# Residual sums of seven of the eight pairs move from VectorE to GpSimd in two RMS-norm transitions of a two-block fp32 kernel

## What is computed

```python
m = jnp.concatenate([a, p], axis=-1) @ w_o[l]
x = x + rms_norm(m, post_mix_g[l])          # transition 1
h = rms_norm(x, pre_ffn_g[l])
up = causal_dwconv(h @ w_up[l], conv_w[l], conv_b[l])
y = (jax.nn.gelu(up[..., :D_FF], approximate=True) * up[..., D_FF:]) @ w_down[l]
x = x + rms_norm(y, post_ffn_g[l])          # transition 2
# second block:
xx = jnp.pad(x, ((0, 0), (1, 0), (0, 0)))[:, :-1] - x
xs = x[None] + xx[None] * mu_proj[:, None, None, :]
proj = jnp.einsum('sbtd,sde->sbte', xs, w_in)
```

## Time and profile before

| what | value |
|---|---|
| median of the runs (2199.85 to 2202.3) | 2200.96 us |
| the profiled execution's own time | 2203.91 us |
| its span, first to last instruction | 2202.1 us |
| TensorE busy | 2155.0 us (98%) |
| VectorE busy | 1486.4 us (67%) |
| ScalarE busy | 1080.2 us (49%) |
| GpSimd busy | 89.5 us (4%) |
| mean granted TensorE clock | 0.992 |

### The profile page before, as it was taken

The page is one execution under the profiler, slowest core; times in us unless marked ns, Lnnn a source line. Parts: engine busy times, 40 slices in busy tenths (PEclk is TensorE's granted clock), DMA queues, the critical chain, the costliest instruction groups (busy, mean ns, idle before and its releaser), DMA issues.

```text
span 2202.1 us, 38428 instructions
## 1 busy us (share of the span) xinstructions
PE 2155.0 (98%) x14720; PEld 1844.7 (84%) x14720; DVE 1486.4 (67%) x2059; ACT 1080.2 (49%) x1521; POOL 89.5 (4%) x78
## 2 busy tenths in 40 slices
PE   9999999999999999999899999999899999999997
PEld 7888888888888888888788888887788888888886
DVE  6556558886488866786786389884676544566655
ACT  5444555444444443444644666544434544556533
POOL 0700000000000000000000000001210000000000
PEclk9999999999999999999999999999999999999998
DMA  8655545665666656655455566653454655654552
GB/s 287 205 168 156 165 148 176 189 190 184 189 190 189 187 187 190 186 175 171 150 175 184 173 180 177 208 167 83 131 172 138 192 189 192 183 153 148 168 183 85
DMA packets 399585, 383.35 MB, mean 174 GB/s; under 512 B 43497, under 2 KB 397345, under 8 KB 398625
## 3 DMA queue, kind: packets, MB, share of 16 engines
q1 hardware_dynamic: 399458, 381.58, 56.1%
HBM read 374.65 MB, written 6.87 MB: 173 GB/s over the span
## 4 chain that ended last, share of the span: by engine, by line
PE 87%; DVE 8%; issue 2%; ACT 2%; DMA 1%; POOL 0%; DVEq 0%; SPq 0%; ACTq 0%; POOLq 0%
PE acc L800 46%; PE acc L803 23%; PE acc L831 3%; PE acc L886 2%; PE acc L887 2%; PE acc L888 2%; PE aux L1155 2%; DVE w_lo L2093 2%; PE acc L834 1%; PE aux L1081 1%; PE aux L903 1%; PE aux L1101 1%; ACT w_hi L1464 0%; DVE inverse L2529 0%; PE aux L1388 0%
## 5 line engine op out<-in xcount | busy, mean ns | idle before, releaser
L2093 DVE TENSOR_TENSOR w_lo<-raw_w,w_hi 128x1024 fp32r<-128x1024 f32 (+1 forms) x592 | 713.1, 1224 | 456.5 <-ACT w_hi L1464 454.8
L1464 ACT ACTIVATE w_hi<-raw_w 128x1024 fp32r<-128x1024 f32 (+1 forms) x592 | 613.5, 1046 | 673.2 <-PE acc L803 574.6
L800 PE MATMUL acc<-h,w_hi 128*128 128x512 f32 x1664 | 525.8, 397 | 1.2 <-DVE w_lo L2093 1.2
L803 PEld LDWEIGHTS acc<-h,w_lo 128*128 128x128 f32 x1664 | 312.6, 188 | 73.8
L803 PE MATMUL acc<-h,w_lo 128*128 128x256 f32 x1664 | 327.0, 278 | 0.0
L800 PEld LDWEIGHTS acc<-h,w_hi 128*128 128x128 f32 x1664 | 254.5, 189 | 2.2 <-issue 1.4
L800 PE MATMUL acc<-ff,w_hi 128*128 128x512 f32 x704 | 222.8, 398 | 2.4 <-DVE ff L2350 2.4
L800 PE MATMUL acc<-x_split,w_hi 128*128 128x512 f32 x704 | 225.1, 401 | 0.0
L800 PE MATMUL acc<-xs_b,w_hi 128*128 128x512 f32 x512 | 162.3, 398 | 1.7 <-DVE w_lo L2538 0.9
L803 PEld LDWEIGHTS acc<-ff,w_lo 128*128 128x128 f32 x704 | 133.0, 189 | 31.5
L803 PEld LDWEIGHTS acc<-x_split,w_lo 128*128 128x128 f32 x704 | 132.2, 188 | 31.2
(11 more groups left out here) (384 smaller groups left out, 3068.2 us busy)
## 6 DMA issues: line engine op xcount, KB each, us to landing
raw_w<-in_w_up SPq DMA_DIRECT2D x176, 512.0 KB, 3.5
raw_w<-in_a_w_in SPq DMA_DIRECT2D x128, 512.0 KB, 4.1
raw_w<-in_w_in SPq DMA_DIRECT2D x64, 512.0 KB, 4.1
raw_w<-in_w_down SPq DMA_DIRECT2D x64, 512.0 KB, 3.6
raw_w<-in_b_w_qg SPq DMA_DIRECT2D x64, 512.0 KB, 3.8
raw_w<-in_w_o SPq DMA_DIRECT2D x32, 512.0 KB, 3.6
raw_w<-in_a_w_out SPq DMA_DIRECT2D x32, 512.0 KB, 3.7
raw_w<-in_w_k_shared SPq DMA_DIRECT2D x32, 512.0 KB, 4.5
```

The costliest lines, as they stand in the source:

```text
L800: pe.matmul(ACC[2 * b + f], WHI[:, q, k, f * P:(f + 1) * P], op[:, kt, :, :].rearrange("p h t -> p (h t)"), start=first, stop=False)
L803: mm = pe.matmul(ACC[2 * b + f][:, 0:T], WLO[:, slot, k, f * P:(f + 1) * P], op[:, kt, 0, :], start=False, stop=last)
L1464: act.activation(WHI[:, u % 4, 0:ku, :], RAWW[:, u, 0:ku, :], ACT.Copy).then_inc(hi_made, 1)
L2093: dve.tensor_tensor(WLO[:, u, 0:ku, :], RAWW[:, u, 0:ku, :], WHI[:, u % 4, 0:ku, :].bitcast(F32), ALU.subtract)\
```

## The change

The product of Y and the scale stays on VectorE for all pairs, and so does the sum of pair 0. For pairs 1 to 7 of both transitions VectorE no longer waits for its product and no longer adds; the product counts a semaphore, and GpSimd, which gets a loop of 2 x 7 sums between the bias and the column of ones, waits for that count, adds, and counts `x_ready`. The semaphore is that of the attention's probabilities, which stands at 8 by then. Nobody else's waits change: ScalarE, TensorE and the DMA queue still count `x_ready` and what follows from it.

```diff
@@ the semaphores @@
-        maxed, expd, probs = sem("maxed"), sem("exp_done"), sem("probs_ready")
+        maxed, expd, probs = sem("maxed"), sem("exp_done"), sem("probs_ready_then_y_by_root")
+        y_normed, HEADS_BEFORE = probs, 8
@@ GpSimd's program, after the bias @@
+            for which in range(2):
+                for p_ in range(1, 8):
+                    x2 = X[:, 2 * p_:2 * p_ + 2, :]
+                    pool.wait_ge(y_normed, HEADS_BEFORE + 7 * which + p_)
+                    pool.tensor_tensor(x2, x2, Y[:, 2 * p_:2 * p_ + 2, :], ALU.add).then_inc(x_ready, 1)
@@ VectorE's add_pair @@
                 dve.wait_ge(y_scaled, seen(y_scaled))
-                link(dve.tensor_tensor(y2, y2, AUX[2][:, 0:T].unsqueeze(1).broadcast_to([P, 2, T]), ALU.mult))
-                dve.tensor_tensor(x2, x2, y2, ALU.add).then_inc(x_ready, 1)
+                normed_y = dve.tensor_tensor(y2, y2, AUX[2][:, 0:T].unsqueeze(1).broadcast_to([P, 2, T]), ALU.mult)
+                if p_:
+                    normed_y.then_inc(y_normed, 1)
+                else:
+                    link(normed_y)
+                    dve.tensor_tensor(x2, x2, y2, ALU.add).then_inc(x_ready, 1)
```

## The result

The changed kernel takes 2209.22 us (median of 6 runs, 2206.34 to 2211.5) beside 2201.18 us for the kernel before in the same series (6 runs, 2199.85 to 2202.59). The ratio is 1.0033, with an interval of 1.0022 to 1.0043: 4.8 to 9.5 us slower. The forecast of 2207.9 lies in that interval, and the time in the range given. A repeat in a later series gave 1.0026 (1.0017 to 1.0035).

The account below looks back on a forecast made before the run. TensorE was taken to bound transition 1, with 0.06 us spare behind VectorE's last sum, and VectorE transition 2. Losses of +3.5 and +3.4 give +6.9 us, from the median 2200.96 to 2207.9, range 2204.5 to 2211.5.

Parts of the forecast that it names:

- The mechanism: VectorE and GpSimd instructions that both read two SBUF tensors exclude each other, about 1.1 us of a GpSimd sum.
- The saving: On VectorE, the next instruction starts 0.61 after a product instead of 1.33: 0.72 us per moved sum, 5.0 per transition.
- Transition 1: Sum of pair 7, then the squares and TensorE, come 3.5 us late: +3.5 us.
- pair 1 to pair 2 (GpSimd first): Transition 1: GpSimd starts first and holds pair 0's low part, so the product of pair 2 starts 0.58 us later.
- pair 2 to 7, five turns: Transition 1: GpSimd slips between the low part's halves, holding the second 1.10: net +0.38 a pair, +1.9.
- product of pair 7 to the sums of squares: End of transition 1: pair 7's sum ends 2.4 us after its product's start instead of 1.41, +1.0.
- Transition 2: VectorE sets the pace: +0.55 after pairs 1, 2, 3, 5, +0.36 after 4, 6, 7, 0.1 waiting: +3.4 us.
- The sum: Both transitions' losses together: +6.9 us.
- Rival 1: No hold, engines work side by side: transition 1 0, transition 2 -1.7, time 2199.2 us; chance 0.09.
- Rival 2: TensorE's clock falls after a longer pause in one of the transitions, costing 3.2 us more: 2211.1; chance 0.12.
- Rival 3: GpSimd's sums more often find VectorE waiting for ScalarE, half the holds hidden: 2.2 us per transition, 2205.4; chance 0.09.

Follow-up runs that it names:

- the last kernel: Against the kernel before, GpSimd sums only pair 1 beside VectorE's products of pairs 2 and 3; other sums on VectorE, a product behind: 2200.07 us, ratio 0.9986.
- the kernel with the fills: Changed kernel with two GpSimd fills of 0.61 us, only writing, in place of each of the 14 sums, which are not made: 2201.79 us, ratio 0.9984.
- the two kernels with and without reads: Kernel before, all sums on VectorE; beside them GpSimd adds two different Y pairs into a spare tile (2216.56 us) or only fills it twice (2202.49 us).
- the one with the product ahead: Kernel before without GpSimd sums; VectorE computes the next pair's product ahead of each sum: 2200.33 us, ratio 0.9987.
- transition 2 alone: Changed kernel with the seven sums on GpSimd only in transition 2, transition 1 as before: 2207.57 us, ratio 1.0016.
- the fill beside: Kernel before, all sums kept on VectorE; beside them GpSimd fills a spare tile twice per moved pair: 2202.49 us, ratio 0.9999.
- transition 1 alone: Changed kernel with the seven sums on GpSimd only in transition 1, transition 2 as before: 2206.6 us, ratio 1.0011.

## Why the prediction came out as it did

**The mechanism** was right. VectorE and GpSimd hold each other off when both read two SBUF tensors; a write by GpSimd holds nobody (shown by the fills), and a VectorE instruction whose second input is the PSUM bank isn't held. The last is shown by the last kernel, whose three products go on at 0.60 each beside a sum; in the changed kernel no product of Y falls beside a sum of GpSimd, so that their 0.68 there says nothing on it. The Trainium skill, "SBUF — State Buffer", section "Who interferes with whom", states the same conditions for VectorE, and beside the two-port modes it has the second engine blocked for the whole instruction. Here the trace differs a little: at 1078.49 GpSimd starts, and VectorE's low part begins as if at 1078.63 + 1.67 - 0.68 = 1079.62, which is 1.13 later, of GpSimd's 1.26. With the whole instruction the loss would have been up to 2 us larger.

**The saving** of 0.72 a sum was right: a low part that waits for nobody starts 0.60 behind the start of the product (319.30 and 319.90), where with the sum between them it is 1.33 (333.39 and 334.72 in the earlier trace rows). In the kernel with the fills, where nothing is held, transition 2 gains.

**Transition 1** was forecast at +3.5 and measured +2.90: a term a fifth too large. Its steps, from product to product against the earlier trace rows and the rows between them:

| step | forecast | measured |
|---|---|---|
| pair 1 to pair 2 (GpSimd first) | +0.58 | +0.52 |
| pair 2 to 7, five turns | +0.38 each, +1.9 | +0.32, +0.30, +0.54, +0.30, +0.31, in all +1.8 |
| product of pair 7 to the sums of squares | +1.0 | +0.6 |

The turn of pair 4 costs 0.54 because GpSimd came first there too (326.05, VectorE at 326.06). The step that failed is the last one, "a wait of 0.1 for ScalarE, 0.38 for the half before it and 1.27". In the timeline the low part, which waits for ScalarE, starts at 335.83 and GpSimd's sum at 335.81: it came 0.02 us ahead of the half that I had put before it, and took 1.30. Who comes first is decided by hundredths of a microsecond, and it moved 0.4 us. The sums of squares started 2.9 us late and not 3.5.

**Transition 2** was forecast at +3.4 and measured +3.26, with the order as worked out: +0.51, +0.56, +0.59 and +0.57 after pairs 1, 2, 3 and 5 (forecast 0.55), +0.30 and +0.31 after 4 and 6 and +0.42 from 7 on (forecast 0.36 each and 0.1). TensorE took all of it, as said: nothing came back in the projection behind.

**The sum** is 6.2 in the traces where I had 6.9. The medians give +8.0 in the first series and +5.6 in the repeat, and both intervals hold 6.2. That the forecast of the time came within 1.3 us of the first median is in part luck, since its terms add up to 0.7 more than the traces show and the median of that series lies 1.8 above them.

**The rivals.** Rival 1, no hold, is refuted by the two kernels with and without reads. But its working can be compared with the kernel that has the fills: 0 and -1.7 forecast, -1.01 and -1.65 measured. Its transition 2 was right. Of transition 1 it said that TensorE stays the bound, which hangs on the clock. TensorE's rows over 312 to 324 in the kernel with the fills, and in the one with the product ahead:

```profile
312.00:324.00 12.00, 10.77 (x60) 8.92 (x60) 7.83 (x15) 6.82 (x14) 4.09 (x7) 1.00 0.13 43
```

```profile
312.00:324.00 12.00, 11.54 (x49) 9.55 (x48) 8.95 (x17) 6.63 (x14) 0.00 (x0) 0.72 0.11 36
```

At 1.00 TensorE is ahead and waits for the chain over VectorE and ScalarE, so that a shorter chain counts (-1.01); at 0.72, the clock of the profile that I read, TensorE is the bound as I said, but by the 0.06 us alone. Where transition 1 is unchanged and the clock was 0.86 (the kernel with transition 2 alone, the fill beside), TensorE waited about 1 us for the squares, and T1 was the same 21.7. The change itself makes the chain longer than either, which is why its T1 is +2.90, +2.87 and +2.92 at clocks of 0.86, 1.00 and 1.00 (over 312 to 324; the changed kernel, transition 1 alone, the repeat). Rival 2, a fall of the clock, was partly right: no fall in the first profile behind 338 or 1078, two in the repeat's transition 2, worth 1.55 us together and not the 3.2 I had put on one. The first cost nothing, since TensorE waits for VectorE behind it and only waited less; the second cost 1.5, where VectorE next needed TensorE's result. Rival 3, less lost by the order of who comes first, is what took 0.4 us out of the last step, far from its 2.5.

What stays open: why a pause of TensorE is followed by a fall of the clock in one execution and by none in another, and whether the kernel with the product ahead gains more at a better clock; no profile of it with one was taken.

## What to carry to other kernels

- Before giving GpSimd elementwise work, look at what VectorE does in the same microseconds, and not at GpSimd's idle share. Beside VectorE instructions with two SBUF inputs, a GpSimd instruction that reads SBUF costs VectorE nearly its own duration: here 1.04 held against 0.72 saved.
- The one sum on GpSimd beside VectorE products that read PSUM was free here, and so were fills in all 14 places. Look in the trace for rows that are longer than their kind, and for what ran on the other engine then: three such rows in another stage, and one that kept its time, were enough to price this change.
- Where two dependent instructions stand back to back on one engine, put an independent one between them first: here that gave as much as the best use of GpSimd did, without it.

## What the runs showed of the hardware that I had not expected

- On GpSimd the sum of a 128x512 fp32 tensor with itself took 0.24 us less than that of two tensors at the same place (rows of 1.48 and 1.72, the wait for VectorE included). The hold of VectorE went with it: 0.79 and 1.03.
- A waiting GpSimd instruction slips in between two instructions of VectorE that stand in its queue one behind the other (319.90, 1086.66): the hold does not last over a row of such instructions.
- The granted clock after equal pauses is not the same. At the second pause of transition 2 the repeat had 2.10 us and a fall, the first profile 2.11 and none; at the first one 2.5, 3.2 and 5.0 us were followed by a fall in three executions, and 3.0 us by none in three others. In the profile of before, a pause of 1.83 us at 1003 was followed by a fall, and the same 1.83 in both profiles of the changed kernel by none. Its rows in before, in the timeline and by stretch:

```profile
1003.01 0.74 PE L800 MATMUL acc<-ff,w_hi 128*128 128x512 f32 x2 [1.83 <-DVE ff L2350]
```

```profile
1005.00:1010.00 5.00, 5.00 (x25) 4.33 (x24) 2.81 (x4) 0.85 (x1) 0.00 (x0) 0.80 0.28 82
```

So a difference of some microseconds between two single profiles of this kernel can be the clock alone, and a length can be compared only where the clock has been looked at.
